# Latent attention: dividing by the softmax sums after the value product, with queries in the rows of that product

## The chip, the cores and the metric

One core of a Trainium2 chip runs the kernel. The metric is device time in microseconds (us); the runs of the kernel before are 2098.66, 2099.0 and 2093.48, their median 2098.66.

## The reference

Two layers, each with a half-step feed-forward block, a mixing stage and a second half-step feed-forward block, for 512 prompt positions and 64 sample positions, 576 tokens in all. The mixing stage projects the tokens to 1824 columns and runs three head groups on them: a chunk MLP (A), sliding-window attention (B), and latent attention (C, four heads). The change lies in C:

```python
def mla_attend(q_lat, q_pe, ckv, kpe, mask):
    s = (jnp.einsum('...qhr,...kr->...hqk', q_lat, ckv)
         + jnp.einsum('...qhp,...kp->...hqk', q_pe, kpe)).astype(jnp.float32) * ((C_NOPE + C_ROPE) ** -0.5)
    if mask is not None:
        s = jnp.where(mask, s, NEG)
    p = jax.nn.softmax(s, axis=-1).astype(ckv.dtype)
    return jnp.einsum('...hqk,...kr->...qhr', p, ckv)
...
    c = jnp.einsum('bthr,hrv->bthv', c_lat, w_uv).reshape(B, T, C_HEADS * C_V)
```

After it `h = h + concat(A, B, C) @ w_out`. The prompt's mask is block-causal in chunks of 64; the sample reads 256 cached positions and its own 64.

## The kernel before

All matrix products of the projections are made in three parts (high by high, low by high, high by low) of fp32r, with TensorE streaming 288 tokens a record. The feed-forward blocks hold most of the time. The change touches only `mixing`, of which each engine has one function (ScalarE L1195, TensorE L1595, VectorE L2361). All three walk the same list of steps, `PLAN` (L166), and each engine emits its own part of every step in that order; so an engine's instructions stand in the order of the list, and wait on counters of the others (`pe_did`, `act_did`, `dve_did`). A number after @ is the pair of PSUM banks, of four, that the step writes; a step waits until the last step in its pair has been read out (`tensor_needs`, L292).

The steps that matter here:
- z:x projects one slot of columns. w:x is ScalarE's making of the high part of a weight slot (L846), after which GpSimd makes the low part (L793). A:n and B:n are products of the output projection with the results of A and B; a B step is 24 TensorE records of 288 tokens. After the list comes `c_part` (L1745), 96 such records, the output projection of the latent attention's result.
- Latent attention runs in units 0 to 9: a tile of queries and a pair of heads. The tiles come in the order 1, 3, 4, 2, 0, with 2, 4, 3, 3 and 1 blocks of keys; tile 4 is the sample with 64 queries, the others have 128.
- MS:n, scores. TensorE makes them with queries in rows (L1699, L1704). VectorE masks (L2487), takes the maximum (L2494) and scales it (L2511). ScalarE takes the exponential for each of the two heads and their sums `den` (L1303). VectorE takes 1/den (L2515) and multiplies the probabilities by it (L2526).
- MT:n turns the probabilities, block by block, so that keys are in rows (TensorE L1713, one record per block and head); ScalarE copies them to one of two buffers `probsT` (L1206).
- MO:n, value product. For each block of keys and head the projected values `vc_tok` (128 keys by 64) stand in the array and the turned probabilities stream through, 128 queries a record, two records per product; the heads fill the two halves of the output's rows (L1736). ScalarE copies the result to `mixed_high` (L1206), VectorE takes the rest to `mixed_low` (L2536). The value product so comes out with channels in rows, as `c_part` reads it.
- The S, T, O steps do the same for the sliding window, with a division of their own that stays as it is.

```python
mm = nc.tensor.matmul(ps[p][64 * j:64 * j + 64, 0, 0:nq], vc_tok[0:n, row, c],
                      probsT[buffer_of(step)][0:n, (2 * k + j) * nq:(2 * k + j + 1) * nq],
                      start=k == 0, stop=k == len(keys) - 1)
```

Of the kernel before, what the change touches and what calls it, by code (L numbers as in the profile page):

```python
# [165 lines left out]
PLAN = """w:q0 z:k@0 sumx@3 w:q1 z:v@1 sw:k tw@2 w:q2 z:q0@0 rot:k z:q1@1 sw:q0 w:q3 w:va0 w:va1 sw:q1 tc@2 w:u0 rot:q0  # L166
z:q2@3 sw:q2 rot:q1 z:q3@1 rot:q2 sw:q3 w:u1 z:va0@0 tk@2 w:ckv w:cq0 rot:q3 z:va1@3 tva:0@0 S:0@2 z:u0@3 tv@1
tva:1@0 a:0@3 T:0@1 S:1@2 z:u1@0 w:cq1 O:0@1 w:cq2 T:1@2 S:2@0 z:ckv@3 T:2@2 w:kpe S:3@3 z:cq0@1 O:1@0 sumkv@3
T:3@1 S:4@2 O:2@3 a:1@1 z:cq1@0 w:qn T:4@3 S:5@1 O:3@2 z:cq2@0 O:4@3 T:5@1 S:6@2 z:kpe@0 sumq@3 tckv@1 O:5@0
T:6@3 w:A0 rkv@1 S:7@2 rep@1 qp@3 vc:0@0 rot:kpe@1 T:7@0 S:8@3 w:A1 qn:0@2 O:6@1 A:0@0 kn:0@3 T:8@2 S:9@1 O:7@0  # L170
A:2@2 qn:1@3 w:B0 A:1@1 rot:qp@0 T:9@2 tkpe@1 O:8@3 O:9@2 A:4@1 MS:0@2 vc:1@1 kn:1@3 w:B1 A:3@2 A:7@3 MT:0@0 w:B2
MS:1@1 B:0@0 A:6@3 MT:1@2 A:5@0 MS:2@3 MO:0@1 B:1@2 B:2@0 MT:2@1 MS:3@2 MO:2@1 B:3@0 MO:1@3 MT:3@2 w:B3 MS:4@1
B:4@3 MO:3@2 MT:4@1 MS:5@0 B:5@1 MT:5@2 MS:6@3 B:6@0 w:C0 MO:4@1 w:C1 MT:6@2 MS:7@3 B:7@1 MO:5@3 MT:7@2 MS:8@0
MO:6@2 MT:8@0 MS:9@2 MO:8@1 MO:7@0 MT:9@2 MO:9@0""".split()
# [2466 lines left out]
```

## Time and profile before

| | |
|---|---|
| runs | 2098.66, 2099.0, 2093.48 us |
| the profiled execution, its own time | 2092.16 us |
| its span | 2090.4 us |
| mean granted clock of TensorE | 0.994 |
| TensorE busy | 2048.2 us, 98% |
| VectorE, ScalarE, GpSimd busy | 1681.3, 977.5, 359.9 us |

The sum of a prediction is made against the profiled execution; of its 1.8 us beside the span the trace tells nothing. The first mixing stage lies at about 417 to 659 us of the span, the second at about 1446 to 1686 us. TensorE's clock has two levels; 1.00 in a row is 2.4 GHz and 0.50 is 1.2 GHz. A record's duration reaches past the start of the next one, since TensorE works in a pipeline; what a record costs is read from start to start.

### The profile page before, as it was taken

The numbers are of one execution on the slowest core, as the hardware profiler recorded it, in microseconds if no ns is written. First come the engines' busy times: TensorE is split into PE (matmuls) and PEld (weight loads), VectorE is DVE, ScalarE is ACT, GpSimd is POOL, SyncE is SP. The second block draws the span as 40 slices with busy tenths as digits, with TensorE's granted clock in tenths as the row PEclk, the third lists the DMA queues.
The fourth block names the chain that finished last, engine by engine and source line by source line (L and its number), as shares of the span: only waits on it lengthen the run. The fifth ranks groups of instructions, "written<-read, shape, count | busy, mean of one in ns | idle before, by whom it ended". The sixth has DMA issues, their size and how long they took to land. (4 is left out here: it accounts for less than half of the span.)

```text
span 2090.4 us, 41116 instructions
## 1 busy us (share of the span) xinstructions
PE 2048.2 (98%) x15435; PEld 1978.9 (95%) x15435; DVE 1681.3 (80%) x2481; ACT 977.5 (47%) x1772; POOL 359.9 (17%) x219
## 2 busy tenths in 40 slices
PE   9999999999999999999999999999999899999998
PEld 7999999999778999999989999999987699999998
DVE  5999998655655999998889999975565579999975
ACT  6544453324535544463465654533344464444532
POOL 0322200141110222200023222002402112222000
PEclk9999999999999999999999999999999999999999
DMA  4223323351111233232223322325312023332231
GB/s 131 94 88 100 96 75 105 94 128 42 46 41 62 86 95 100 91 92 85 77 82 101 100 80 87 103 76 128 94 45 64 31 62 101 100 93 85 83 105 64
DMA packets 236727, 178.35 MB, mean 85 GB/s; under 512 B 35808, under 2 KB 231616, under 8 KB 236608
## 3 DMA queue, kind: packets, MB, share of 16 engines
q1 hardware_dynamic: 231712, 170.36, 27.4%
q10 hardware_dynamic: 4896, 6.36, 1.1%
q8 instruction: 80, 1.31, 0.3%
q14 instruction: 39, 0.32, 0.1%
HBM read 170.12 MB, written 3.62 MB: 83 GB/s over the span
## 5 line engine op out<-in xcount | busy, mean ns | idle before, releaser
L1437 PE MATMUL pair<-t_parts,chunk_high 128*128 128x288 f32 x4592 | 919.2, 296 | 5.2 <-POOL chunk_low L799 2.5
L1437 PEld LDWEIGHTS pair<-t_parts,chunk_high 128*128 128x128 f32 x4592 | 738.9, 189 | 6.6 <-POOL chunk_low L799 3.2
L1437 PE MATMUL pair<-t_parts,chunk_low 128*128 128x288 f32 x2296 | 678.9, 296 | 0.0
L1437 PEld LDWEIGHTS pair<-t_parts,chunk_low 128*128 128x128 f32 x2296 | 432.7, 188 | 0.0
L799 POOL TENSOR_TENSOR chunk_low<-set_raw,chunk_high 128x512 fp32r<-128x512 f32 x164 | 237.5, 1458 | 871.5 <-ACT chunk_high L898 871.5
L898 ACT ACTIVATE chunk_high<-chunk_sum 128x512 fp32r<-128x512 f32 x328 | 203.9, 631 | 373.4 <-DVE chunk_sum L1990 190.3
L2002 DVE TENSOR_TENSOR chunk_low<-chunk_sum,chunk_high 128x512 fp32r<-128x512 f32 x328 | 214.4, 694 | 9.2 <-ACT chunk_high L898 1.9
L793 POOL TENSOR_TENSOR w_low<-raw,w_high 128x1024 fp32r<-128x1024 f32 (+2 forms) x48 | 115.0, 2402 | 619.6 <-ACT w_high L846 619.6
L1384 PE MATMUL pair<-hidden_high,w_high 128*128 128x288 f32 x896 | 192.1, 296 | 0.0
L1384 PE MATMUL pair<-hidden_high,w_low 128*128 128x288 f32 x896 | 191.9, 296 | 0.0
L1384 PE MATMUL pair<-hidden_low,w_high 128*128 128x288 f32 x896 | 191.6, 296 | 0.0
L846 ACT ACTIVATE w_high<-raw 128x896 fp32r<-128x896 f32 (+2 forms) x112 | 110.1, 984 | 140.5 <-PE pair L1570 56.0
L898 ACT ACTIVATE chunk_high<-set_raw 128x512 fp32r<-128x512 f32 x246 | 149.3, 620 | 0.0
L1384 PEld LDWEIGHTS pair<-hidden_low,w_high 128*128 128x128 f32 x896 | 144.5, 189 | 0.0
L1384 PEld LDWEIGHTS pair<-hidden_high,w_high 128*128 128x128 f32 x896 | 144.2, 189 | 0.0
L1384 PEld LDWEIGHTS pair<-hidden_high,w_low 128*128 128x128 f32 x896 | 144.2, 189 | 0.0
L1384 PE MATMUL pair<-x_high,w_high 128*128 128x288 f32 x480 | 105.1, 300 | 0.0
L1384 PE MATMUL pair<-x_high,w_low 128*128 128x288 f32 x480 | 102.7, 296 | 0.0
L1384 PE MATMUL pair<-x_low,w_high 128*128 128x288 f32 x480 | 102.6, 295 | 0.0
L1985 DVE TENSOR_TENSOR chunk_sum<-set_raw 128x512 f32<-128x512 f32 x82 | 82.4, 1005 | 14.9 <-PE pair L1437 14.5
L1021 ACT ACTIVATE chunk_high<-chunk_sum 128x512 fp32r<-128x512 f32 x64 | 39.1, 633 | 110.5 <-DVE chunk_sum L1910 95.2
L926 ACT ACTIVATE outputs<-outputs 128x576 f32<-128x576 f32 x88 | 59.4, 686 | 59.9 <-DVE outputs L2071 59.6
(300 smaller groups left out, 3732.6 us busy)
## 6 DMA issues: line engine op xcount, KB each, us to landing
set_raw<-in_w_up_dram SPq DMA_DIRECT2D x44, 1024.0 KB, 5.3
set_raw<-in_w_gate_dram SPq DMA_DIRECT2D x44, 1024.0 KB, 5.3
raw<-in_w_down_dram SPq DMA_DIRECT2D x64, 448.0 KB, 3.8
down_raw<-in_w_down_dram SPq DMA_DIRECT2D x16, 1024.0 KB, 5.4
raw<-in_w_in_dram SPq DMA_DIRECT2D x20, 512.0 KB, 4.0
raw<-in_w_in_dram SPq DMA_DIRECT2D x16, 256.0 KB, 3.8
raw<-in_w_out_dram SPq DMA_DIRECT2D x8, 512.0 KB, 3.5
raw<-in_w_out_dram SPq DMA_DIRECT2D x16, 256.0 KB, 4.0
```

Of the source, the lines that this page charges most:

```text
L793: nc.gpsimd.tensor_tensor(**low_of(s, slot_size(s))).then_inc(low_ready, 1)
L799: nc.gpsimd.tensor_tensor(out=cl[:, j], in0=set_raw[b][:, :, int(j == A12), 0:P], in1=ch[:, j].bitcast(F32), op=ALU.subtract).then_inc(low ...
L846: nc.scalar.activation(wh[s % RING][:, 0:n], raw[s % RAW][:, raw_from(s):raw_from(s) + n], ACT.Copy).then_inc(high_ready, 1)
L898: nc.scalar.activation(ch[:, j], src, ACT.Copy).then_inc(chunk_high, 1)
L926: nc.scalar.activation(g, g, ACT.Silu).then_inc(silu_done, 1)
L1021: nc.scalar.activation(ch[:, down_unit(g, j)], src, ACT.Copy).then_inc(d_high, 1)
L1384: mm = nc.tensor.matmul(ps[p][:, half, 0:HALF], w, x[:, half * HALF:(half + 1) * HALF], start=first and k == 0 and q == 0, stop=last and k ...
L1437: mm = nc.tensor.matmul(out, c[:, j, p, :], tr[p // 2][:, seat(p), x, t, :], start=p == 0 and n == 0, stop=p == KP - 1 and n == 2)
L1985: ins = nc.vector.tensor_tensor(cf[:, S1], block(b, 0, 1), block(b, 1, 1), ALU.add)
L2002: nc.vector.tensor_tensor(cl[:, j], src, ch[:, j].bitcast(F32), ALU.subtract).then_inc(low_by_dve, 1)
```

## The change

MS no longer multiplies the probabilities: VectorE writes 1/den to `inv_latent`, a column per unit and head, and is done. MT waits for ScalarE's exponentials instead of VectorE. MO has its operands exchanged: the turned probabilities stand in the array and 64 values stream through, with queries in rows and the two heads side by side in columns. ScalarE copies each head's half, multiplied by `inv_latent`, to one of two new tiles `o_tok`. A new step MU turns that tile (one TensorE record) and ScalarE and VectorE read it out as they read MO before. `PLAN` is another list: MU steps come in, and other steps and pairs are placed anew.

```diff
-MO:6@2 MT:8@0 MS:9@2 MO:8@1 MO:7@0 MT:9@2 MO:9@0""".split()
+MT:7@2 w:C0 MS:8@0 w:C1 MU:5@3 MO:6@2 B:7@1 MT:8@3 MS:9@2 MO:8@1 MU:6@3 MO:7@0 MT:9@2 MU:8@1 MO:9@0 MU:7@0 MU:9@2""".split()
...
+        "MT": lambda: [scalar_ops(f"MS:{arg}")[-1]],
+        "MU": lambda: [scalar_ops(f"MO:{arg}")[-1]],
...
-        "MT": lambda: [vector_ops(f"MS:{arg}")[-1]],
...
+        inv_latent = mix("inv_latent", [P, 2 * UNITS])
+        o_tok = [mix(f"o_tok{j}", [P, P]) for j in range(2)]
...
                     elif kind == "MO":
                         i, pair, t0, nq, keys = mla_unit(arg)
+                        dve_did(act, layer, vector_end(f"MS:{arg}"))
+                        turn = [x for x in MIX if x[:3] == "MO:"]
+                        at_n = turn.index(step)
+                        if at_n >= 2:
+                            pe_did(act, layer, "MU" + turn[at_n - 2][2:])
+                        for j in range(2):
+                            copy(o_tok[at_n % 2][0:nq, 64 * j:64 * j + 64], ps[p][0:nq, 0, 64 * j:64 * j + 64], f"{step}.{j}",
+                                 scale=inv_latent[0:nq, 2 * arg + j:2 * arg + j + 1])
+                    elif kind == "MU":
+                        i, pair, t0, nq, keys = mla_unit(arg)
                         copy(mh[:, 6 + pair, t0:t0 + nq], ps[p][:, 0, 0:nq], f"{step}.0")
...
-                        for k, (tile, n) in enumerate(keys):
-                            row = tile if i < 4 else (4, 5, 6)[k]
-                            for j in range(2):
-                                c = slice((2 * pair + j) * C_V, (2 * pair + j + 1) * C_V)
-                                mm = nc.tensor.matmul(ps[p][64 * j:64 * j + 64, 0, 0:nq], vc_tok[0:n, row, c],
-                                                      probsT[buffer_of(step)][0:n, (2 * k + j) * nq:(2 * k + j + 1) * nq],
-                                                      start=k == 0, stop=k == len(keys) - 1)
+                        for j in range(2):
+                            c = slice((2 * pair + j) * C_V, (2 * pair + j + 1) * C_V)
+                            for k, (tile, n) in enumerate(keys):
+                                row = tile if i < 4 else (4, 5, 6)[k]
+                                mm = nc.tensor.matmul(ps[p][0:nq, 0, 64 * j:64 * j + 64], probsT[buffer_of(step)][0:n, (2 * k + j) * nq:(2 * k + j + 1) * nq],
+                                                      vc_tok[0:n, row, c], start=k == 0, stop=k == len(keys) - 1)
+                    elif kind == "MU":
+                        i, pair, t0, nq, keys = mla_unit(arg)
+                        turn = [x for x in MIX if x[:3] == "MO:"]
+                        mm = nc.tensor.transpose(ps[p][:, 0, 0:nq], o_tok[turn.index(f"MO:{arg}") % 2][0:nq, :], ident[0:nq, 0:nq])
...
+                        if not swa:
+                            emit(nc.vector.reciprocal(inv_latent[0:nq, 2 * arg:2 * arg + 2], den[0:nq, 0:2]), names[n])
+                            continue
...
-                            emit(nc.vector.tensor_tensor(pr, pr, inv, ALU.mult), names[n])
```

TensorE at the end of the list, before: the last rows of the value product MO:5, then MT:7, MS:8 (two rows), MO:6, MT:8, MS:9 (two rows), MO:8, MO:7, MT:9 and MO:9. The step B:7 stands just ahead of these rows.

```order
L1736 MATMUL pair<-probsT_102,vc_tok 64x64 x6
L1713 MATMUL pair<-ident,probs 128x128 x6
L1699 MATMUL pair<-k_nopeT_132,q_nopeT_134 128x128 x2
L1704 MATMUL pair<-kpeT,q_peT 128x128 x2
L1736 MATMUL pair<-probsT_101,vc_tok 64x128 x6
L1713 MATMUL pair<-ident,probs 128x128 x2
L1699 MATMUL pair<-k_nopeT_133,q_nopeT_135 128x128 x2
L1704 MATMUL pair<-kpeT,q_peT 128x128 x2
L1736 MATMUL pair<-probsT_101,vc_tok 64x128 x2
L1736 MATMUL pair<-probsT_102,vc_tok 64x128 x6
L1713 MATMUL pair<-ident,probs 128x128 x2
L1736 MATMUL pair<-probsT_102,vc_tok 64x128 x2
```

The same place in the changed kernel, in two pieces. First from MS:7 to MO:6, behind which B:7 now stands (L1712 and L1717 are MS, L1749 is MO, L1726 is MT, L1754 is the new MU):

```order
L1712 MATMUL pair<-k_nopeT_134,q_nopeT_136 128x384 x2
L1717 MATMUL pair<-kpeT,q_peT 128x384 x2
L1749 MATMUL pair<-vc_tok,probsT_102 64x64 x6
L1726 MATMUL pair<-ident,probs 128x128 x6
L1712 MATMUL pair<-k_nopeT_133,q_nopeT_135 128x128 x2
L1717 MATMUL pair<-kpeT,q_peT 128x128 x2
L1754 MATMUL pair<-ident,o_tok_146 128x64
L1749 MATMUL pair<-vc_tok,probsT_101 128x64 x6
```

B:7 has moved from between MS:7 and MT:7 to between MO:6 and MT:8. Then, behind B:7, to the end of the list:

```order
L1726 MATMUL pair<-ident,probs 128x128 x2
L1712 MATMUL pair<-k_nopeT_134,q_nopeT_136 128x128 x2
L1717 MATMUL pair<-kpeT,q_peT 128x128 x2
L1749 MATMUL pair<-vc_tok,probsT_101 128x64 x2
L1754 MATMUL pair<-ident,o_tok_145 128x128
L1749 MATMUL pair<-vc_tok,probsT_102 128x64 x6
L1726 MATMUL pair<-ident,probs 128x128 x2
L1754 MATMUL pair<-ident,o_tok_146 128x128
L1749 MATMUL pair<-vc_tok,probsT_102 128x64 x2
L1754 MATMUL pair<-ident,o_tok_145 128x128
L1754 MATMUL pair<-ident,o_tok_146 128x128
```

Every value product is followed, one or more steps later, by its turn, and the list ends on two turns. ScalarE at the same place, before, from the exponentials of MS:8 on:

```order
L1303 ACTIVATE probs,den<-pair,neg_max,q_scale 128x128 x2
L1206 ACTIVATE mixed_high<-pair 128x128
L1206 ACTIVATE probsT_101<-pair 128x256
L1303 ACTIVATE probs,den<-pair,neg_max,q_scale 128x128 x2
L1206 ACTIVATE mixed_high<-pair 128x128 x2
L1206 ACTIVATE probsT_102<-pair 128x256
L1206 ACTIVATE mixed_high<-pair 128x128
```

And now, from the exponentials of MS:9 on:

```order
L1306 ACTIVATE probs,den<-pair,neg_max,q_scale 128x128 x2
L1209 ACTIVATE o_tok_146<-pair,inv_latent 128x64 x2
L1209 ACTIVATE mixed_high<-pair 128x128
L1209 ACTIVATE o_tok_145<-pair,inv_latent 128x64 x2
L1209 ACTIVATE probsT_102<-pair 128x256
L1209 ACTIVATE mixed_high<-pair 128x128
L1209 ACTIVATE o_tok_146<-pair,inv_latent 128x64 x2
L1209 ACTIVATE mixed_high<-pair 128x128 x2
```

Five copies stand between the last exponentials and the copy of `probsT` that MO:9 waits for, where two stood.

## Rows read from the trace of the kernel before

**Rows 1.** The page, part 1: busy time by engine.
```profile
PE 2048.2 (98%) x15435; PEld 1978.9 (95%) x15435; DVE 1681.3 (80%) x2481; ACT 977.5 (47%) x1772; POOL 359.9 (17%) x219
```
**Rows 2.** Waits of PE: line, releaser, us in total, times, longest.
```profile
PE pair L1713 <- DVE probs L2526: 10.5, 10, 2.0
PE pair L1713 <- issue: 4.0, 6, 1.1
...
PE pair L1384 <- DVE mixed_low L2536: 1.8, 2, 0.9
...
PE pair L1649 <- ACT ckvT L1206: 1.5, 2, 0.9
PE pair L1721 <- DVE z L2409: 1.4, 1, 1.4
PE pair L1721 <- ACT roots L1263: 1.4, 1, 1.4
...
PE pair L1736 <- ACT probsT L1206: 0.9, 2, 0.5
```
**Rows 3.** Timeline of PE, first layer, MO:5 to c_part: start, length in us.
```profile
631.37 0.71 PE L1736 MATMUL pair<-probsT,vc_tok 128*64 128x64 f32 x12
632.61 0.84 PE L1713 MATMUL pair<-ident,probs 128*128 128x128 f32 x6 [0.53 <-issue]
633.38 0.49 PE L1699 MATMUL pair<-k_nopeT,q_nopeT 64*128 64x128 f32 x4
...
644.70 0.82 PE L1384 MATMUL pair<-mixed_high,w_high 128*128 128x288 f32 x2 [0.89 <-DVE mixed_low L2536]
```
**Rows 4.** Timeline of PE, second layer, MS:8 to c_part.
```profile
1662.15 0.49 PE L1699 MATMUL pair<-k_nopeT,q_nopeT 64*128 64x128 f32 x4
...
1665.96 0.41 PE L1713 MATMUL pair<-ident,probs 128*128 128x128 f32 x2 [1.97 <-DVE probs L2526]
...
1667.17 1.09 PE L1736 MATMUL pair<-probsT,vc_tok 128*64 128x128 f32 x16
...
1672.36 0.82 PE L1384 MATMUL pair<-mixed_high,w_high 128*128 128x288 f32 x2 [0.89 <-DVE mixed_low L2536]
```
**Rows 5.** Timeline of PE: three stretches with full-precision records, first layer.
```profile
533.03 1.15 PE L1631 MATMUL pair<-mean_d,sq_tmp 128*128 128x1 f32 x10
...
574.64 0.33 PE L1682 MATMUL pair<-ckvT,w_uk 128*128 128x64 f32 x2
574.78 0.51 PE L1384 MATMUL pair<-mixed_high,w_high 128*128 128x288 f32 x2
...
599.82 1.09 PE L1736 MATMUL pair<-probsT,vc_tok 128*64 128x128 f32 x16
```
**Rows 6.** Timeline of PE, first layer: B:4 with the start of MO:3 behind it.
```profile
607.40 0.53 PE L1384 MATMUL pair<-mixed_high,w_high 128*128 128x288 f32 x2
...
610.78 0.44 PE L1736 MATMUL pair<-probsT,vc_tok 128*64 128x128 f32 x4
```
**Rows 7.** Timelines of PE (end of MS:6's scores) and ACT (exponentials, copies), both layers.
```profile
620.01 0.91 PE L1704 MATMUL pair<-kpeT,q_peT 32*128 32x384 f32 x4
...
623.84 0.20 ACT L1303 ACTIVATION_READ_ACCUMULATOR probs<-pair,neg_max,q_scale 128x1 f32 x1
...
641.11 0.44 ACT L1206 ACTIVATE mixed_high<-pair 128x128 fp32r<-128x128 f32 x2
642.67 0.38 ACT L1206 ACTIVATE probsT<-pair 128x256 f32<-128x256 f32 x1 [1.12 <-PE pair L1713]
...
1669.19 0.20 ACT L1303 ACTIVATION_READ_ACCUMULATOR probs<-pair,neg_max,q_scale 128x1 f32 x1
```
**Rows 8.** Windows: busy by engine (PE, PEld, DVE, ACT, POOL), then PEclk, DMA, GB/s.
```profile
638.00:644.00 6.00, 4.33 (x30) 2.71 (x27) 1.99 (x7) 1.88 (x9) 0.00 (x0) 0.50 0.01 3
1664.00:1666.00 2.00, 0.04 (x1) 0.07 (x2) 0.81 (x4) 1.16 (x5) 0.00 (x0) 1.00 0.00 0
1666.00:1668.00 2.00, 2.00 (x26) 1.59 (x26) 0.73 (x3) 0.38 (x1) 0.00 (x0) 1.00 0.00 0
```

More of the change, by code:

```diff
@@ L165 @@
 MLA_TILES = [1, 3, 4, 2, 0]
[L166 to L173, printed above, removed]
-MO:6@2 MT:8@0 MS:9@2 MO:8@1 MO:7@0 MT:9@2 MO:9@0""".split()
+PLAN = """w:q0 z:k@0 sumx@3 w:q1 z:v@1 sw:k tw@2 w:q2 z:q0@0 sw:q0 rot:q0 w:q3 rot:k z:q1@2 w:va0 tc@0 sw:q1 z:q2@3 w:va1
+w:u0 sw:q2 rot:q1 z:q3@1 rot:q2 tk@2 z:va0@0 sw:q3 w:u1 rot:q3 z:va1@3 tva:0@0 w:ckv S:0@2 w:cq0 z:u0@3 tv@2
+tva:1@1 a:0@3 w:cq1 T:0@1 S:1@0 w:cq2 z:u1@3 O:0@1 T:1@2 S:2@0 z:ckv@1 T:2@0 w:kpe S:3@2 z:cq0@1 sumkv@3 O:1@0
+T:3@1 S:4@2 O:2@3 a:1@1 z:cq1@0 T:4@3 S:5@1 O:3@2 z:cq2@0 w:qn O:4@3 T:5@1 S:6@2 z:kpe@0 sumq@3 w:A0 tckv@2 O:5@0
+T:6@3 rkv@1 S:7@2 rep@1 qp@3 vc:0@0 rot:kpe@1 T:7@0 S:8@3 qn:0@2 O:6@1 A:0@0 w:A1 kn:0@3 T:8@2 S:9@1 O:7@0 qn:1@3
+A:2@2 A:1@1 rot:qp@0 T:9@2 w:B0 w:B1 O:8@3 tkpe@1 O:9@2 A:4@0 MS:0@3 vc:1@1 kn:1@0 A:3@2 MT:0@3 MS:1@1 B:0@0
+A:6@2 A:7@3 MO:0@1 MT:1@2 A:5@0 w:B2 MU:0@2 MS:2@1 MO:1@3 B:1@2 B:2@0 MT:2@1 MS:3@2 MO:2@1 B:3@0 MU:2@1 MU:1@3
+w:B3 MT:3@2 MS:4@1 B:4@2 MT:4@1 MS:5@0 MO:3@3 B:5@1 MT:5@2 MS:6@3 B:6@2 MO:4@1 MT:6@2 MU:3@3 MU:4@1 MS:7@0 MO:5@1
+MT:7@2 w:C0 MS:8@0 w:C1 MU:5@3 MO:6@2 B:7@1 MT:8@3 MS:9@2 MO:8@1 MU:6@3 MO:7@0 MT:9@2 MU:8@1 MO:9@0 MU:7@0 MU:9@2""".split()
 MIX = [t.partition("@")[0] for t in PLAN]
@@ L213, in scalar_ops @@
     n = {"z": 0, "sumx": 1, "sumkv": 2, "sumq": 4, "tw": 1, "tv": 2, "tc": 2, "tk": 2, "tva": 2,
-         "rkv": 2, "tkpe": 2, "rep": 1, "a": 1, "kn": 1, "S": 5, "O": 1, "MS": 2, "MO": 1}.get(kind, 0)
+         "rkv": 2, "tkpe": 2, "rep": 1, "a": 1, "kn": 1, "S": 5, "O": 1, "MS": 2, "MO": 2, "MU": 1}.get(kind, 0)
     if kind == "vc":
@@ L231, in vector_ops @@
     n = {"z": 1, "sumx": 2, "sumq": 3, "tckv": 2, "tw": 1, "rot": 3, "a": 4, "qp": 1, "qn": 1,
-         "O": 1, "MO": 1, "A": 1, "B": 1}.get(kind, 0)
+         "O": 1, "MU": 1, "A": 1, "B": 1}.get(kind, 0)
     if kind == "z" and arg.startswith("cq"):
@@ L237, in vector_ops @@
     if kind == "MS":
-        n = 4 + (1 if mla_unit(arg)[0] < 4 else 0)
+        n = 3 + (1 if mla_unit(arg)[0] < 4 else 0)
     return [f"{step}.{k}" for k in range(n)]
@@ L265, in evacuated @@
     kind, arg = split(step)
-    if kind in ("z", "qp", "qn", "O", "MO", "A", "B"):
+    if kind in ("z", "qp", "qn", "O", "MU", "A", "B"):
         return "vector", f"{step}.0"
@@ L1300, in mixing @@
                         W = sum(n for _, n in keys)
-                        dve_did(act, layer, f"{step}.{len(vector_ops(step)) - 3}")
+                        dve_did(act, layer, f"{step}.{len(vector_ops(step)) - 2}")
                         for j in range(2):
@@ L1754, in c_part @@
                     if m == 0:
-                        dve_did(pe, layer, max((f"MO:{n}.0" for n in range(UNITS)), key=DVE_STEPS.index))
+                        dve_did(pe, layer, max((f"MU:{n}.0" for n in range(UNITS)), key=DVE_STEPS.index))
                     if m >= 4:
@@ L2519, in mixing @@
                         inv = inv_den[0:nq, 0:heads].unsqueeze(2).broadcast_to([nq, heads, W])
-                        if swa:
-                            emit(nc.vector.tensor_tensor(pr[:, 0:2], pr[:, 0:2], inv[:, 0:2], ALU.mult), names[n])
-                            n += 1
-                            emit(nc.vector.tensor_tensor(pr[:, 2:4], pr[:, 2:4], inv[:, 2:4], ALU.mult), names[n])
-                        else:
-                            emit(nc.vector.tensor_tensor(pr, pr, inv, ALU.mult), names[n])
+                        emit(nc.vector.tensor_tensor(pr[:, 0:2], pr[:, 0:2], inv[:, 0:2], ALU.mult), names[n])
+                        n += 1
+                        emit(nc.vector.tensor_tensor(pr[:, 2:4], pr[:, 2:4], inv[:, 2:4], ALU.mult), names[n])
                     elif kind == "O":
@@ L2532, in mixing @@
                                                      mh[:, js, t0:t0 + nq].bitcast(F32), ALU.subtract), names[0])
-                    elif kind == "MO":
+                    elif kind == "MU":
                         i, pair, t0, nq, keys = mla_unit(arg)
```

1 line of the change is left out of this document (removed).

## The prediction

> **What bounds the kernel.** I read the page first: TensorE is busy for 98% of the span, VectorE for 80%, ScalarE for 47% [rows 1]. So work taken from VectorE is worth only what TensorE waited for it, and every record added to TensorE counts, unless it falls into a wait. Then I read TensorE's waits. MT waits 10.5 us in ten places for the multiplication of the probabilities. "Issue" ahead of L1713 is 4.0 us in six: I take the two of 1.1 us for the sliding window's T:5 (one a layer) and the other 1.8 us for MT. The last value product waits 0.9 us for `probsT`, and `c_part` 1.8 us for `mixed_low` [rows 2]. Together 15.0 us in latent attention, 7.5 a layer: that is all the change can win there. The last view is the timeline of the end of each list. There TensorE has no projection product left to fill in, and from MS:8 to the first record of `c_part` it takes 644.70 - 633.38 = 11.3 us in the first layer [rows 3] and 1672.36 - 1662.15 = 10.2 us in the second [rows 4]. The reader should see in both that over half of the 15 us stands in this stretch.
>
> **The value product, MO.** Two products a key block, one per head, two records each. Before, 16 records take 1.09 us, 0.068 each [rows 5]: the two heads use different halves of the array's columns, 64 columns stand and 128 stream. After, 128 columns stand and 64 stream. No row has just this in a long series. Two rows bound it. Ten records with 128 standing columns and a single streamed one take 1.15 us, 0.115 each; that cannot be the streaming. Two records of exactly the new shape (L1682, 128x64) are followed after 0.14 us by the next product, 0.070 each, though behind a long record, under which their loads may hide [rows 5]. I take 0.115, since in MO no long record hides the loads; 0.070 stays as the lower end, at which the exchange costs nothing. In a layer the four tiles with 128 queries have 10 key blocks, so 10 x 2 pairs x 2 heads x 2 = 80 records: 80 x 0.047 = 3.8 us. Tile 4 stays at 64 standing columns; 0.
>
> The Trainium skill says, in TensorE: Matmul & The Clock Gate, section LDWEIGHTS, that a load of the standing operand costs time by its columns and not by its rows, 107 ns for 128 as I work it out from its formula. By it alone the exchange would cost 80 x (0.107 - 0.068) = 3.1 us a layer; the row with one streamed column agrees with it, the 0.14 us of the two records doesn't.
>
> **The turn, MU.** Ten records a layer. Six turns of MT take 633.38 - 632.61 = 0.77 us, 0.13 each [rows 3]; 1.2 us a layer, 0.6 of it up to MT:7. All of them stand beside other small steps, so no new change between kinds of products is paid.
>
> **VectorE and ScalarE.** VectorE loses a multiplication a unit, ScalarE gains two copies of 128x64 for one. Between them the steps A and B cover this, up to MS:7; at nothing, with this cover: behind MS:4, for instance, stands B:4, 610.78 - 607.40 = 3.4 us [rows 6]. From the end of the scores of a tile with three blocks (0.91 us from 620.01) to its last exponential's end (624.04) is 3.1 to 3.2 us [rows 7]. With a B step between MS and MT, MT then finds its exponentials done. I find this for MT:1 to MT:6, so the waits up to MT:7 vanish: 10.5 us less the four long ones of MT:8 and MT:9 (1.97, 1.0, 1.97, 1.88, of which [rows 4] show one), so 3.7, and the 1.8 us of issue; 5.5, or 2.8 a layer. The loads and low parts of the last weight slots come up to 8 us later; the first use of the feed-forward's first set lies behind three tiles of `c_part`, which covers that.
>
> **What takes their place.** B:7 stood between MS:7 and MT:7 and has moved behind MO:6. Between MS:7 and MT:7 is left only MO:5, 0.7 us [rows 3], against 3.2 us: a new wait of 2.5 us at MT:7.
>
> So from the start of latent attention to the end of MT:7, per layer: -3.4 (B:7 gone) - 2.8 + 2.3 (48 records of MO:0 to MO:3) + 0.6 + 2.5 = -0.8 us.
>
> **The end, from MS:8 on,** set out from 0:
> - MS:8 0.9, MU:5 0.1, MO:6 12 x 0.115 = 1.4, B:7 3.4: 5.8. MT:8 waits for nothing. MT:8 and MS:9 take 1667.17 - 1665.96 = 1.2 [rows 4]: 7.0.
> - MT:9 needs the exponentials of MS:9, which end 1669.39 - 1667.17 = 2.2 after it [rows 4, 7]: 9.2. MO:8, MU:6 and MO:7 are 2.0 us of work and lie within.
> - On ScalarE five small copies stand ahead of MT:9's copy. Two take 0.44 [rows 7], a further one about 0.2: 10.2. MT:9's copy takes 0.38: MO:9 starts at 10.7.
> - MO:9 four records and their drain, 0.6; two copies 0.5; MU:7 and MU:9 with drain 0.5; two copies 0.45; VectorE's rest and the signals 0.4: `c_part` starts at 13.1.
>
> Against 11.3 and 10.2 us: +1.8 and +2.9. So most of what the last turns and copies add lies on the path: MO to MU to `c_part` is a chain with nothing beside it.
>
> **Clock.** In the first layer the granted clock is 0.50 from 638 to 644 us, after a wait of 2 us. In the second, TensorE does 0.04 us of work from 1664 to 1666, has 1.00 all the same to 1668 [rows 8]. I leave what the clock costs in either layer as it was.
>
> **Sum.** First layer -0.8 + 1.8, second -0.8 + 2.9: together +3.1 us. The steps in front of latent attention keep their waits: 0. Ends: if MO's records cost 0.070, 160 x 0.045 = 7.2 us go: -4.1. Against the profiled execution: 2092.2 + 3.1 = 2095.3 us. This execution lies 6.5 us under the median of the runs, and of the four times two are near 2093 and two near 2099; their middle is 2095.6, and I forecast 2095.6 + 3.1, about 2098 us. A measurement tells this kernel from no change at about 0.3%, 6 us; so the forecast is: no change that counts.
>
> **Rivals.**
> - *Loads hidden.* The records of MO cost 0.070, as the two of L1682 do. Against it: the 0.115 of the short ones. -4.1 us, 2092.
> - *The front.* The list is new there too: w:A0 now stands ahead of the copies that `rep` (L1649) waits for, `w:qn` later. The waits in front are 2.2 us of T:5, 1.5 and twice 1.4 [rows 2], 6.5 in both layers. If they go, 3.1 - 6.5 = -3.4 us, 2092. Against it: `rep`'s successor waits for the same exponentials of S:7, so a wait taken from `rep` comes back one step later.
> - *Slower: the clock.* The new wait of 2.5 us at MT:7 is as long as the one after which the first layer ran at 0.50 for 6 us and more. If the clock falls there and stays down to the end of the list, the 7 us of work from MS:8 to MS:9, B:7 among them, take 14: one layer +7, 2106 us; both, 2113. It decides whether 0.50 stands in the windows before B:7. For it: [rows 8], first layer; against it: the second layer, where the same wait was followed by the full clock.
> - *The doing itself.* Should MT still wait for VectorE, through the pair or the list, the 5.5 us stay: +8.6, 2104. The order of the instructions speaks against it; I give it almost nothing.
>
> **Chances.** Forecast 0.53; loads hidden 0.14; the front 0.12; clock 0.14; the rest, among it two gains at once (-10.6 us) and a clock that doesn't fall at `c_part`, 0.07. Faster by over 0.3% are the two gains at once and the outer parts of each, 0.17; slower by over 0.3% are the clock and a little of the forecast's own scatter, 0.16; within, 0.67. The range: the scatter of the runs, 2092 to 2099, with -4.1 below gives 2088, and with one layer's clock above, 2106.
>
> **What would show it.** In the profile after: L1749 near 0.115 us a record; no wait of L1726 for VectorE; a wait of about 2.5 us ahead of MT:7 for ScalarE and one below 0.5 at MT:9; waits ahead of the last MO, the last MU and `c_part`; some 13 us from MS:8 to `c_part`. The forecast is wrong if MO's records come at 0.07, if 0.50 stands in front of B:7, or if the time between the end of the first product block and latent attention changes by over 2 us.

## The result and the profile after

The changed kernel takes 2110.82 us (median of 4 runs, 2107.51 to 2111.45), the kernel before 2096.87 us (4 runs, 2093.48 to 2099.0): a ratio of 1.0067, 95% interval 1.0053 to 1.0081, 14 us slower. The forecast was 2098 us with a range from 2088 to 2106: wrong, and above the range. The profiled execution took 2107.51 us with a span of 2105.3, against 2092.16 and 2090.4 before, so 14.9 us lie between the two traces.

The page, part 1, of the changed kernel: TensorE gained 16 us of busy time for 20 records, VectorE lost 10 [rows 1].

```profile
PE 2064.5 (98%) x15455; PEld 1998.1 (95%) x15455; DVE 1671.2 (79%) x2461; ACT 985.0 (47%) x1812; POOL 358.7 (17%) x219
```

TensorE's waits after (line, releaser, us in total, times, longest), to be held against [rows 2]:

```profile
PE pair L1726 <- ACT probs L1306: 4.5, 4, 2.0
...
PE pair L1726 <- issue: 2.5, 3, 1.2
...
PE pair L1668 <- ACT kpe_rep L1209: 2.1, 2, 1.0
PE pair L1397 <- DVE mixed_low L2550: 2.0, 2, 1.0
...
PE pair L1726 <- DVE probs L2540: 1.5, 1, 1.5
PE pair L1685 <- DVE uT L2425: 1.4, 2, 0.7
...
PE pair L1754 <- ACT o_tok L1209: 1.2, 2, 0.6
...
PE pair L1749 <- ACT probsT L1209: 1.0, 2, 0.5
...
PE pair L1726 <- DVE z L2425: 0.6, 2, 0.3
PE pair L1675 <- ACT probs L1298: 0.6, 2, 0.3
```

The 10.5 us for VectorE behind the scores are gone. In latent attention MT waits 4.5 us for the exponentials: 1.96 in each layer at MT:7 and 0.30 at MT:9. The last MO, the last MU and `c_part` wait as the walk had it. But L1685 and L1675 waited for nothing before, and L1668 has 2.1 us where the same line (L1655) had 0.9, while `rep`'s 1.5 us are gone [rows 2]: all of these are in front of latent attention (L1726 waits for VectorE there too, since T and MT share the line).

The timeline of PE in the first layer, MO:5 to `c_part` (start, length, operation), answers to [rows 3]:

```profile
630.81 1.30 PE L1749 MATMUL pair<-vc_tok,probsT 128*64 128x64 f32 x12
634.08 0.85 PE L1726 MATMUL pair<-ident,probs 128*128 128x128 f32 x6 [1.96 <-ACT probs L1306]
634.85 0.49 PE L1712 MATMUL pair<-k_nopeT,q_nopeT 64*128 64x128 f32 x4
...
635.90 2.75 PE L1749 MATMUL pair<-vc_tok,probsT 128*128 128x64 f32 x12
638.40 0.83 PE L1397 MATMUL pair<-mixed_high,w_high 128*128 128x288 f32 x2
...
643.65 0.38 PE L1726 MATMUL pair<-ident,probs 128*128 128x128 f32 x2
...
645.42 1.45 PE L1749 MATMUL pair<-vc_tok,probsT 128*128 128x64 f32 x12
647.17 0.41 PE L1726 MATMUL pair<-ident,probs 128*128 128x128 f32 x2 [0.30 <-ACT probs L1306]
...
648.33 0.66 PE L1749 MATMUL pair<-vc_tok,probsT 128*128 128x64 f32 x4 [0.52 <-ACT probsT L1209]
649.60 0.67 PE L1754 MATMUL pair<-ident,o_tok 128*128 128x128 f32 x2 [0.61 <-ACT o_tok L1209]
651.26 0.82 PE L1397 MATMUL pair<-mixed_high,w_high 128*128 128x288 f32 x2 [0.99 <-DVE mixed_low L2550]
```

The same twelve records of a value product stand there twice: 2.75 us at 635.90, behind the wait, and 1.45 us at 645.42. B:7, from 638.40 to 643.65, takes 5.25 us instead of 3.4. The windows say why. The last three columns are the granted clock, the DMA share and GB/s; the first four windows are of the first layer, the last two of the second:

```profile
636.00:640.00 4.00, 4.00 (x19) 4.00 (x20) 1.15 (x5) 3.17 (x9) 3.21 (x2) 0.50 0.02 4
640.00:644.00 4.00, 4.00 (x23) 3.83 (x22) 0.08 (x1) 0.00 (x0) 1.48 (x1) 0.65 0.21 58
...
648.00:652.00 4.00, 2.06 (x9) 1.56 (x10) 1.43 (x5) 1.46 (x7) 0.00 (x0) 0.71 0.00 0
652.00:656.00 4.00, 4.00 (x19) 4.00 (x18) 0.76 (x1) 0.55 (x2) 0.00 (x0) 0.50 0.00 0
...
1668.00:1672.00 4.00, 3.95 (x19) 3.08 (x19) 0.84 (x4) 2.06 (x4) 0.56 (x1) 0.50 0.00 0
...
1684.00:1688.00 4.00, 2.50 (x9) 2.13 (x10) 1.12 (x3) 0.94 (x4) 0.00 (x0) 0.50 0.01 4
```

Twice in each layer the clock goes down to 1.2 GHz (0.50) in place of 2.4: behind the wait at MT:7, and behind the small waits at the end of the list, where `c_part` begins. In four of the six windows TensorE is busy for 3.95 us or more of the 4, so the low clock lies over work. In the kernel before, the low clock of the first layer lay for the most part over windows in which TensorE had less to do (2.33 us of 4 here):

```profile
640.00:644.00 4.00, 2.33 (x16) 1.16 (x12) 1.30 (x5) 1.85 (x8) 0.00 (x0) 0.50 0.00 0
```

Cut at the same records (first token sum, MS:0, MS:8, first record of `c_part`, and the feed-forward's first record behind it), the layers look so, in us, with four of the experiments told below. The shifted kernel has other steps between MS:0 and MS:8 than the rest, so for it only the sum of the two middle stretches compares:

| stretch, layer | before | after | idle products at MT:7 | B:7 back | shifted | before, idle products |
|---|---|---|---|---|---|---|
| token sums to MS:0, first | 152.9 | 154.5 | 155.9 | 154.5 | 154.3 | 153.0 |
| the same, second | 152.9 | 154.8 | 154.8 | 154.9 | 152.9 | 154.1 |
| MS:0 to MS:8, first | 63.0 | 61.9 | 61.9 | 63.2 | 57.0 | 63.1 |
| second | 63.0 | 62.5 | 61.9 | 63.2 | 57.0 | 63.1 |
| MS:8 to `c_part`, first | 11.3 | 16.4 | 13.2 | 14.7 | 15.3 | 11.0 |
| second | 10.2 | 16.7 | 13.2 | 14.7 | 15.3 | 11.0 |
| `c_part`, first | 14.3 | 15.2 | 15.6 | 15.6 | 12.9 | 12.8 |
| second | 13.9 | 14.9 | 15.3 | 14.2 | 12.9 | 12.8 |

From before to after: front +1.6 and +1.9, MS:0 to MS:8 -1.2 and -0.5, the end +5.1 and +6.5, `c_part` +0.9 and +1.0: 15.3 us. What is left of the 14.9 is -0.4: a low clock in the first 40 us of this execution, 1.1, against 1.5 us less between the two layers.

### The profile page after: what moved, and what is told of

The parts are those of the page before. It is cut to its first block and busy times, and to the rows that moved or that the text cites. A ratio compares the mean times of both kernels' runs of the same rounds, so it can differ in the third digit from the quotient of the medians.

```text
span 2105.3 us, 41202 instructions
## 1 busy us (share of the span) xinstructions
PE 2064.5 (98%) x15455; PEld 1998.1 (95%) x15455; DVE 1671.2 (79%) x2461; ACT 985.0 (47%) x1812; POOL 358.7 (17%) x219
## 3 DMA queue, kind: packets, MB, share of 16 engines
q8 instruction: 80, 1.31, 0.3%
## 5 line engine op out<-in xcount | busy, mean ns | idle before, releaser
L2001 DVE TENSOR_TENSOR chunk_sum<-set_raw 128x512 f32<-128x512 f32 x82 | 83.9, 1023 | 14.2 <-PE pair L1450 13.8
```

The costliest lines, as they stand in the source:

```text
L2001: ins = nc.vector.tensor_tensor(cf[:, S1], block(b, 0, 1), block(b, 1, 1), ALU.add)
```

## The experiments

The theory: the walk along the end of the list was right at the full clock (13.1 us), the clock then took some 3 us of each end and more of `c_part`, and the front took the rest. The rivals: the clock would fall there anyway; the new division costs it all; the front is only clock.

**The front.** The changed kernel with the old order up to A:4.

```diff
-PLAN = """w:q0 z:k@0 sumx@3 w:q1 z:v@1 sw:k tw@2 w:q2 z:q0@0 sw:q0 rot:q0 w:q3 rot:k z:q1@2 w:va0 tc@0 sw:q1 z:q2@3 w:va1
...
+PLAN = """w:q0 z:k@0 sumx@3 w:q1 z:v@1 sw:k tw@2 w:q2 z:q0@0 rot:k z:q1@1 sw:q0 w:q3 w:va0 w:va1 sw:q1 tc@2 w:u0 rot:q0 z:q2@3
...
```

> The changed kernel with the old list up to A:4, its own from there on. Theory 1 (the new front of the list costs time): the stretch from the token sums (418.5) to MS:0 (573.0) was 1.6 us longer in the first layer and 1.9 us in the second than before; it goes back, 3.4 us of 2107.5, and the tail is as it was: about 2104 in the profiled execution, 2107 by the median. Theory 2 (the front differs by chance or through the changed steps behind it): the stretch stays 1.6 and 1.9 us longer and the time stays at 2107 to 2111.

Measured: 2106.76 us (4 runs, 2106.15 to 2106.88), 4.1 us less. In the changed kernel's trace the front has four new waits in the first layer:

```profile
473.64 0.74 PE L1675 MATMUL pair<-ident,vT 128*128 128x128 f32 x5 [0.31 <-ACT probs L1298]
475.64 1.36 PE L1685 MATMUL pair<-w_sT,va_tok 128*64 128x128 f32 x20 [0.71 <-DVE uT L2425]
486.07 0.63 PE L1726 MATMUL pair<-ident,probs 128*128 128x128 f32 x4 [0.68 <-issue]
504.80 0.95 PE L1726 MATMUL pair<-ident,probs 128*128 128x128 f32 x7 [0.31 <-DVE z L2425]
```

They are 2.0 us, of which 1.8 remain up to T:5 and 1.6 at MS:0. The trace names VectorE for half of them (`uT`, which step a:0 needs, and `z`). From 440 to 460 us VectorE is busy for 16.9 us where it was busy for 13.4, since `rot:q0`, `rot:k` and `tc` now come to it in another order; with the old order it is busy for 13.5 us there and the four waits are gone. That it is this reordering and none of the others in the front wasn't tested by itself. Yet in the profile of this experiment the stretch takes 154.0 and 154.5 us, hardly less, record for record as before up to `rep` (L1662), then 1.1 us later in the first layer, and 1.5 in the second from T:6 on. One window at that place, of the kernel before and then of the experiment:

```profile
544.00:548.00 4.00, 3.56 (x19) 2.67 (x17) 1.50 (x4) 3.85 (x12) 0.00 (x0) 1.00 0.51 131
```

```profile
544.00:548.00 4.00, 4.00 (x20) 3.85 (x20) 1.11 (x4) 3.31 (x11) 0.00 (x0) 0.72 0.48 131
```

The same program piece at the same times, once with the full clock and once not: behind its two waits of 1.1 and 1.4 us [rows 2] the clock falls in some executions and not in others. The profiled execution of the kernel before had it in neither layer, which may be a part of why it lies 5 us under the median. Over all traces of this document, the old front takes 152.9 to 153.0 us in 12 of 20 layers and 154.0 to 155.3 in the other eight; the new one takes 154.5 to 156.2 in eight layers and never less. So a front is to be judged by its waits, or by many traces, not by its length in one; by the median, this one costs 4 us.

**The clock behind MT:7.** Fifteen idle products (a product into the PSUM pair that MT:7 will overwrite) keep TensorE at work in the wait.

```diff
+                    if step == "MT:7":
+                        act_did(pe, layer, evacuated(before_in_pair(step))[1])
+                        for _ in range(15):
+                            nc.tensor.matmul(ps[p][:, 0, 0:HALF], wh[1][:, 0:P], mh[:, 0, 0:HALF], start=True, stop=True)
```

> The changed kernel with 15 idle products of 128x288 put on TensorE in the wait ahead of MT:7 (about 2.0 us, the length of the wait); they write the bank pair that MT:7 overwrites and delay nothing. Theory 1 (the clock falls because of this wait): 0.50 no longer stands in the windows between MT:7 and MT:8 in either layer, MO:6 and B:7 run at full speed, and 3.1 + 3.3 + 0.7 = 7 us go: about 2100.5 profiled, 2104 by the median. Theory 2 (the clock falls through the exchanged operands or the turns, with the wait as a bystander): 0.50 stands there still and the time stays within 2 us.

Measured: 2100.82 us (10 runs, 2098.92 to 2102.91), 10.0 us less, 3 more than expected: adding work won 10 us. The timeline of PE, first layer, with the idle products (L1619):

```profile
632.45 2.24 PE L1619 MATMUL pair<-mixed_high,w_high 128*128 128x288 f32 x15
...
636.32 1.55 PE L1753 MATMUL pair<-vc_tok,probsT 128*128 128x64 f32 x12
...
648.43 0.82 PE L1397 MATMUL pair<-mixed_high,w_high 128*128 128x288 f32 x2 [1.10 <-DVE mixed_low L2554]
```

MO:6 takes 1.55 us in place of 2.75, B:7 its 3.3, and MS:8 to `c_part` takes 13.15 us in one layer and 13.18 in the other: the 13.1 us of the walk, at full clock. The traces account for 3.3 + 3.5 + 0.6 us of the gain (the last is MT:7 itself in the second layer). The other 2.6 no trace shows; they would fit that the profiled execution of the changed kernel lies 3.3 us under its own median. What the edit doesn't touch is `c_part`: 15.6 and 15.3 us, at half clock behind the small waits.

**B:7 back where it was,** between MS:7 and MO:5; else the changed kernel.

```diff
-w:B3 MT:3@2 MS:4@1 B:4@2 MT:4@1 MS:5@0 MO:3@3 B:5@1 MT:5@2 MS:6@3 B:6@2 MO:4@1 MT:6@2 MU:3@3 MU:4@1 MS:7@0 MO:5@1
...
+MS:5@0 MO:3@3 B:5@1 MT:5@2 MS:6@3 B:6@2 MO:4@1 MT:6@2 MU:3@3 MU:4@1 MS:7@0 B:7@3 MO:5@1 MT:7@2 w:C0 MS:8@0 w:C1 MU:5@3
...
```

> The changed kernel with B:7 back between MS:7 and MO:5, where it stood before. Theory 1 (the place of B:7 makes wait and fall of the clock): the 2.0 us wait ahead of MT:7 is gone, one of 0.5 to 0.9 us stands ahead of MT:8, the 7 us of half clock are gone; per layer -2.0 + 0.7, together -2.6 - 7 = about -9.6 us: 2098 profiled, 2101 by the median. Theory 2 (the end of the list is so thin without B:7 that the clock falls all the same, only later): the waits change as said, but 0.50 stands from about MT:9 or MT:8 on, and only 3 to 6 us are won.

Measured: 2106.05 us (5 runs, 2105.23 to 2106.09), 4.8 us less; the second theory by its size. A wait of 2 us now stands at MT:8, and the clock falls behind it. But it is another wait than the one at MT:7. These are lines of the timelines of ScalarE, VectorE and PE in the first layer, then PE's windows:

```profile
639.56 1.05 ACT L849 ACTIVATE w_high<-raw 128x1024 fp32r<-128x1024 f32 x1
640.50 0.22 ACT L1209 ACTIVATE mixed_high<-pair 128x64 fp32r<-128x64 f32 x1
...
640.85 0.23 DVE L2550 TENSOR_TENSOR mixed_low<-pair,mixed_high 128x64 fp32r<-128x64 f32 x1 [0.99 <-ACT mixed_high L1209]
...
641.18 0.66 PE L1726 MATMUL pair<-ident,probs 128*128 128x128 f32 x2 [1.98 <-ACT o_tok L1209]
```

```profile
640.00:644.00 4.00, 2.82 (x14) 2.08 (x15) 0.72 (x3) 1.51 (x5) 3.19 (x2) 0.54 0.00 0
644.00:648.00 4.00, 3.74 (x19) 3.34 (x18) 0.78 (x4) 2.52 (x11) 0.00 (x0) 0.50 0.81 261
648.00:652.00 4.00, 2.40 (x9) 1.84 (x10) 1.41 (x4) 1.03 (x5) 0.00 (x0) 0.50 0.01 2
```

The exponentials of MS:8 are done at 639.66, so for them MT:8 would have waited some 0.5 us, as expected. The other 1.5 us it waits for its pair of banks, 3, which MU:5 wrote: ScalarE copies that product only behind the weight slot of w:C1 (1.05 us), and VectorE's rest of it ends at 641.08, 0.1 us ahead of MT:8. The trace puts the wait down to a copy of ScalarE that ran at the same time. So putting B:7 back took away the wait at MT:7 and made one of the same length out of a pair and the place of w:C1. What B:7's place is worth by itself this run doesn't show; it does show that a wait of 2 us is followed by the low clock here too, with less of B behind it.

**What the division costs in the kernel before.** Multiplication left out (the probabilities are not divided), MT waits for the exponentials.

```diff
+        "MT": lambda: [scalar_ops(f"MS:{arg}")[-1]],
...
-        "MT": lambda: [vector_ops(f"MS:{arg}")[-1]],
...
+                        if not swa:
+                            continue
                         own(names[n])
```

> The kernel before, its own list, with the multiplication by 1/den left out (the latent attention's values are not divided) and MT waiting for the exponentials. It shows what taking the multiplication off the path is worth by itself. Theory 1 (its waits are worth what the rows said): the waits ahead of MT fall by up to 0.6 to 1.45 us each, in all 3.7 + 1.8 + 4 x 0.65 = about 8 us: 2084 profiled, -8 against before. Theory 2 (a wait that is shortened comes back at the next step, or the weights' steps on ScalarE take it): under 4 us.

Measured: 2086.64 us (4 runs, 2085.17 to 2089.41), 10.3 us less, where 8 were expected. So of the 15.0 us of waits in latent attention about 10 could be won in this order, clock included; and the new records cost 5 us a layer by the forecast, 5.6 as measured below, which is as much or more.

**The new division alone,** on the old order with MU put in (the diff is against the list of the kernel before).

```diff
-MO:6@2 MT:8@0 MS:9@2 MO:8@1 MO:7@0 MT:9@2 MO:9@0""".split()
+MO:6@2 MT:8@0 MS:9@2 MO:8@1 MU:6@3 MO:7@0 MT:9@2 MU:8@1 MO:9@0 MU:7@3 MU:9@2""".split()
```

> The new division alone, on the order of the kernel before, with the MU steps put in (the order that the change searched is left out). If the division alone is nearly free and the new order brought the loss (front of the list, the wait ahead of MT:7, B:7 at half clock), this runs within 3 us of the kernel before: 2096 to 2100. If the new division itself costs what was lost (full-precision loads and the longer end walk at whatever clock), it runs at 2104 or more.

Measured: 2105.28 us (6 runs, 2104.37 to 2106.7): the second case. MS:0 to `c_part` takes 78.7 and 78.5 us against 74.4 and 73.3, `c_part` 15.3 and 15.5. Part of it is the records (5.6 us a layer, as the two shifted kernels show below). The waits, in turn, went only in part; timeline of PE, first layer:

```profile
597.73 1.07 PE L1726 MATMUL pair<-ident,probs 128*128 128x128 f32 x8 [1.18 <-issue]
...
639.83 0.41 PE L1726 MATMUL pair<-ident,probs 128*128 128x128 f32 x2 [1.07 <-ACT probs L1306]
```

Between MS and MT the old order has too little work for the exponentials themselves, whoever divides. The clock is 0.50 to 0.60 from 640 to 652 us and 0.63 or less from 1674 to 1686.

**Idle products in all waits of the end,** on the changed kernel with the old front (15 at MT:7, and 4, 4 and 7 ahead of MO:9, MU:9 and `c_part`), **and the same in the kernel before** (15, 14, 3 and 6 ahead of MT:8, MT:9, MO:9 and `c_part`).

```diff
+            def fill(layer, n, done):
+                engine, name = evacuated(done)
+                (act_did if engine == "scalar" else dve_did)(pe, layer, name)
+                for _ in range(n):
+                    nc.tensor.matmul(ps[3][:, 0, 0:HALF], mh[:, 0, 0:P], mh[:, 0, 0:HALF], start=True, stop=True)
...
+                        fill(layer, 7, 'MU:6')
```

> The changed kernel with the old order up to A:4, 15 idle products in the wait ahead of MT:7 and 4, 4 and 7 idle ones in the waits ahead of the last MO, the last MU and the first product of c_part. Theory (two independent losses: front of the list 4 us, clock 10 us, and a third of about 1 us per layer at the head of c_part): 2110.8 - 4 - 10 - 2 = about 2095, c_part's first four blocks back to 14.0 us per layer, no 0.50 in either tail. Rival (the gains overlap, or the clock falls elsewhere as soon as it is held up here): 2099 or more, with a window of 0.50 further on.

> The kernel before, with 15, 14, 3 and 6 idle products in its own waits ahead of MT:8, MT:9, the last MO and c_part: what a held clock is worth with the division where it was. Theory (the same wait of 1.97 us also lets the clock fall in the old kernel, but with little work behind it): 1.1 us won in the first layer's tail, up to 0.7 in each c_part, so 2094 to 2096, and a gain far below the 10 us that the same edit gave the changed kernel. Rival (holding the clock up is worth the same in either kernel, so the clock is no reason for the loss): 2087 or so.

Measured: 2095.78 us (12 runs, 2093.5 to 2099.5) for the first, 15 us under the changed kernel, where 2095 was expected: front and clock add up. The idle products aren't free, and the clock isn't held everywhere: from MS:8 to `c_part` the first layer takes 15.0 us, with 0.59 from 643 to 647 us, and the second 14.1, at full clock, against 13.2 with MT:7's wait alone filled. And 2091.7 us (10 runs, 2089.87 to 2093.01) for the second, 5.3 us under the kernel before. `c_part` takes 12.8 to 13.0 us in both. So a held clock is worth 11.0 us to the changed kernel with the old front (2106.76 less 2095.78) and 5.3 to the one before, more there than the 1 to 3 expected, and far from equal. By these medians the 14 us of the change are 4.1 of front, 5.7 of clock (11.0 less 5.3) and 4.1 that stay when front and clock are set right (2095.78 less 2091.7). The window of the kernel before with idle products, first layer, over the end of the list:

```profile
633.00:645.00 12.00, 11.02 (x99) 9.30 (x100) 5.35 (x17) 4.34 (x15) 0.00 (x0) 1.00 0.16 55
```

**The B products later.** Instead of idle products, real ones: B:0 goes behind MS:2 in place of MS:1, B:1 behind MS:3 in place of MS:2, and B:2 to B:5 go two units later, B:5 behind MS:7; pairs and weight steps are placed anew with them; B:6 fills the wait ahead of MT:8 and B:7 the one behind MT:9.

```diff
-MT:7@2 w:C0 MS:8@0 w:C1 MU:5@3 MO:6@2 B:7@1 MT:8@3 MS:9@2 MO:8@1 MU:6@3 MO:7@0 MT:9@2 MU:8@1 MO:9@0 MU:7@0 MU:9@2""".split()
...
+B:3@0 MT:5@1 MS:6@2 B:4@0 MO:4@3 MT:6@1 MU:3@0 MU:4@3 w:C0 MS:7@2 MO:5@1 B:5@0 MT:7@1 w:C1 MS:8@3 MU:5@2 MO:6@0 B:6@1
+MT:8@2 MS:9@0 MO:8@3 MU:6@1 MO:7@2 MT:9@0 B:7@3 MU:8@1 MO:9@2 MU:7@0 MU:9@3""".split()
```

> The changed kernel with the old order up to A:4 and, behind it, the B products one unit later than before the change (B:0 behind MS:2 to B:5 behind MS:7), B:6 between MS:8 and MT:8, B:7 between MT:9 and MO:9, so that no wait of 2 us is left ahead of MT:7. Theory (the half clock behind the long wait is most of the loss): no L1726 wait for ScalarE of 2 us, 1.00 in the windows of both tails, median 6 to 10 us below the old-front kernel's 2106.8, so 2097 to 2101. Rival (the clock falls from the density of the short products themselves, wait or no wait): a window of 0.50 in both tails all the same and 2104 to 2107. Second rival (the B products are needed where they were, and waits come back up to MT:7): the stretch from MS:0 to MS:8 grows by over 3 us per layer, 2105 or more.

Measured: 2087.18 us (6 runs, 2085.7 to 2088.42), ratio to the kernel before 0.9956 (0.9944 to 0.9968): 9.9 us faster than before the change, 23.6 than after it, and 10 under the bottom of what was expected. The windows over both ends:

```profile
628.00:644.00 16.00, 14.52 (x113) 12.88 (x111) 5.49 (x16) 7.23 (x26) 2.40 (x1) 1.00 0.22 67
1652.00:1668.00 16.00, 14.36 (x111) 12.84 (x111) 5.67 (x17) 7.13 (x25) 2.39 (x1) 1.00 0.21 67
```

Neither is below 1.00, nor are the windows over the two `c_part`s (644 to 658 us and 1668 to 1682), and MS:0 to `c_part` takes 72.24 us in both layers, 2.8 less than at full clock in the changed order (61.9 + 13.15), the wait at MT:7 and two small ones being filled.

**Is that the order or the division?** The same order without MU on the kernel before (the diff is against its list); and the shifted kernel with the changed kernel's front.

```diff
-MS:1@1 B:0@0 A:6@3 MT:1@2 A:5@0 MS:2@3 MO:0@1 B:1@2 B:2@0 MT:2@1 MS:3@2 MO:2@1 B:3@0 MO:1@3 MT:3@2 w:B3 MS:4@1
...
+w:B2 MS:2@1 MO:1@3 B:0@0 MT:2@1 MS:3@2 MO:2@1 B:1@0 w:B3 MT:3@2 MS:4@1 B:2@0 MT:4@1 MS:5@3 MO:3@2 B:3@0 MT:5@1 MS:6@2
+B:4@0 MO:4@3 MT:6@1 w:C0 MS:7@2 MO:5@1 B:5@0 MT:7@1 w:C1 MS:8@3 MO:6@0 B:6@1 MT:8@2 MS:9@0 MO:8@3 MO:7@2 MT:9@0 B:7@3
+MO:9@2""".split()
```

> The order of the shifted kernel (B products one unit later, B:6 and B:7 in the last two waits), without the MU steps, on the kernel before, whose division stands in front of the turn. Theory (the shift gained by covering waits, whichever the division, and the new division still costs its full-precision records): from the shifted kernel's 72.24 us from MS:0 to c_part go 3.6 us of MO and some 1.5 us of MU, and up to 2 us of waits for VectorE come: 67 to 69 us, c_part 12.9, median 2079 to 2085, so below the 2087.2 of the shifted kernel. Rival (without the new division the turn still waits for VectorE behind each scores step, and the shift pays only with the division moved out of the way): over 71 us from MS:0 to c_part and 2087 to 2093.

> The shifted order from A:4 on, with the changed kernel's own front of the list. Theory (front and rest add up): the front costs here what it cost with the other tail, 4 us, so 2091 (2089.5 to 2092.5), with 154.5 us from the token sums to MS:0. Rival (most of those 4 us were a lower clock that the earlier waits brought on, and go with it): 2088 or less.

Measured: 2089.44 us (6 runs, 2086.93 to 2091.65) with the old division, in the rival's range: its MS:0 to `c_part` takes 72.4 and 73.6 us. What it doesn't pay in MO and MU it waits: in the first layer, at full clock in both, TensorE is busy for 64.6 us where it is busy for 70.2 with the new division, and idle for 7.7 where it is idle for 2.0. Two of its waits, in the second layer:

```profile
1654.47 0.84 PE L1713 MATMUL pair<-ident,probs 128*128 128x128 f32 x6 [1.67 <-DVE mixed_low L2536]
...
1664.31 0.66 PE L1713 MATMUL pair<-ident,probs 128*128 128x128 f32 x2 [1.88 <-DVE probs L2526]
```

With the changed kernel's front the shifted kernel takes 2091.08 us (8 runs, 2090.07 to 2091.86), 3.9 more than without, as expected, though the two ran on different chips; against all 12 runs of the shifted kernel (2088.2, below) it is 2.9. So the front costs about as much with this end as with the other. To tell the two divisions apart, both shifted kernels ran again on one chip:

> The shifted kernel with the new division a second time, now on one chip with the shifted kernel of the old division. Theory (with the B products one unit later the new division pays, since the old one still waits for VectorE in the tail): 2087 again, 1.5 to 3 us below the other, the two sets of runs hardly overlapping. Rival (the 2.3 us between them lay between two chips): both within 1 us.

> The shifted kernel with the old division a second time, beside the one with the new division. Theory: 2089 to 2090, and above the other. Rival: within 1 us of it.

Measured: 2089.36 us (6 runs, 2086.93 to 2090.64) with the new division and 2088.43 us (5 runs, 2087.11 to 2089.78) with the old one. The rival holds. Over both times the medians are 2088.2 (12 runs) and 2088.5 (11 runs): in this order the new division is worth nothing that these runs can tell. All of the gain over the kernel before, 8 to 10 us, is the order's. The traces do differ: with the new division MS:0 to `c_part` takes 72.24 or 72.25 us in all six layers traced, and with the old one 72.4, 73.6, 73.6 and 75.4, the longer ones with a low clock behind waits of 1.67 or 1.88 us (0.61 to 0.70 over 4 us). Why that doesn't reach the medians stays open.

## Why the prediction was wrong, point by point

Two steps failed, both of them terms put at nothing: what the clock costs (8.2 us by the traces, 5.7 by the medians) and the front of the list (3.4 us by the traces, 4 by the median). The rest of the sum came within 0.5 us, in part by luck.

- *The value product.* L1749 has 8 records from 592.55 to the next product at 593.46, 0.114 each, and 16 from 603.02 to 604.83, 0.113:

```profile
592.55 1.10 PE L1749 MATMUL pair<-vc_tok,probsT 128*128 128x64 f32 x8
593.46 0.51 PE L1397 MATMUL pair<-mixed_high,w_high 128*128 128x288 f32 x2
...
603.02 2.00 PE L1749 MATMUL pair<-vc_tok,probsT 128*128 128x64 f32 x16
604.83 0.38 PE L1397 MATMUL pair<-mixed_high,w_high 128*128 128x288 f32 x1
```

  The size is right for the tiles with 128 queries, 0.115 taken, and "loads hidden" is out. The reason is not, or not alone, that 128 columns stand. Tile 4 was put at 0 ("stays at 64 standing columns"), yet its twelve records of one and the same shape went from 0.71 us, 0.059 each [rows 3], to 1.27 in MO:4 and 1.31 in MO:5 (the line at 630.81), 0.105 to 0.109 each. Before, the two heads stood in different halves of the array's columns, and the trace has their records starting two by two, 6 to 7 ns apart. Now both heads use the same columns, and the records start one by one. The first 0.03 us of MO:5 before has two records, the first 0.06 us now has one:

```profile
631.37 0.28 PE L1736 MATMUL pair<-probsT,vc_tok 128*64 128x64 f32 x2
...
630.81 0.24 PE L1749 MATMUL pair<-vc_tok,probsT 128*64 128x64 f32 x1
```

  So the change gave up that TensorE ran two heads side by side, a term the prediction had in view ("the two heads use different halves") and didn't price. With it MO costs 4.5 us a layer at full clock (3.4 for the tiles with 128 queries, 1.1 for tile 4), not 3.8. How much of the 3.4 is width and how much pairing no run separates. The Trainium skill's 107 ns from TensorE: Matmul & The Clock Gate, section LDWEIGHTS, is 6 ns under what the records with 128 standing columns show. By the same formula 64 columns are 53 ns, an estimate; tile 4's records took 59 before and take 105 to 109 now, so columns alone don't set a record's cost here.
- *MU, VectorE and ScalarE.* Right: no MT waits for VectorE's multiplication any more, and MS:0 to MS:8 fell by 1.2 us in the first layer (the forecast had 0.8 up to the end of MT:7) and by 0.5 in the second, where MT:7 at half clock adds 0.6. That the sum is near is partly luck. Taken from start to start, the terms are -4.0 for B:7 (-3.4 forecast), -2.8 for the waits and MT (-2.8), +1.9 for MO:0 to MO:3 (+2.3), +1.1 for tile 4 (0), +0.6 for MU (+0.6) and +2.0 for the wait at MT:7 (+2.5).
- *The new wait at MT:7.* 2.5 us forecast, 1.96 measured. From the end of MS:7's scores to its last exponential are 3.1 us, as forecast; what stands in between, MO:5, takes 1.3 us and not 0.7. So MO:5's extra cost lies in the wait, and only MO:4's lengthens the layer.
- *The walk along the end.* Right: 13.1 us forecast, 13.15 and 13.18 measured once the clock was held. Inside it two small misses cancel: MO:9 starts at 10.35 and not 10.7, and the rest takes 2.8 and not 2.4. At one clock the step from MS:0 to `c_part` thus costs 75.05 - 73.25 = 1.8 us a layer; the sum said 3.1 for both together. But the sum set a walk at full clock against 11.3 us of the first layer, of which 1.1 is half clock, and so took those 1.1 us off without saying so. At one clock its own terms give 4.2, against 3.6 measured.
- *"I leave what the clock costs in either layer as it was."* This step failed, and it is most of the error. Of the 16.4 and 16.7 us of the end, 3.3 and 3.5 are half clock, and 0.6 more at MT:7; `c_part`, which takes 12.9 us at full clock, takes 15.2 and 14.9. That is 11.7 us. In the kernel before it is 1.1 us in the first end and 1.4 and 1.0 in the two `c_part`s, 3.5. So 8.2 of the 15 us. The rival named the mechanism and the place, and its sign (0.50 before B:7) is there in both layers of this trace, and in both of the experiment with the old front; but it had 0.14, and it priced 7 us a layer where the end lost 3.3, because the clock came back inside B:7. It left out `c_part`, where the clock falls a second time and costs 4.4 us in both layers. The argument against it, that the second layer had kept its clock behind the same wait, was one execution of something that varies.
- *"The steps in front of latent attention keep their waits: 0."* This failed too: +1.6 and +1.9 us, 4 by the median. The prediction knew that the list was new there and looked only for waits that might go. What it said of `rep` held: its 1.5 us are gone, and L1668, a step later, waits 1.2 more.
- *The base.* The sum was set on a time 3 us above the profiled execution, rightly: over 59 runs in these comparisons the kernel before has a median of 2097.0 (2092.1 to 2099.9).

So 3.6 (measured at full clock, 3.1 forecast), 8.2 of clock and 3.4 of front make 15.2, against 15.3 between the cuts. The medians with idle products give the clock less, 5.7 us, and the rest 4.1; the idle products' own cost and what varies from execution to execution lie between the two. What else stays open is the 2.6 us of the idle products' gain that the two profiled executions don't show, and why 1.5 us less lie between the layers.

## What to carry to other kernels

Price a wait on a nearly full TensorE by what runs behind it as well as by its length: 2 us of idling cost 2 us and up to 5 us more of half clock, and it was worth 10 us to fill it even with idle work. Hold back independent products for the last waits of a stage, each a unit or two later, before changing how the stage computes: here the order brought 8 to 10 us and the new algorithm, once ordered, nothing. Before exchanging the operands of a product, look whether products run side by side, and price what is lost with that. And where a change brings a newly searched order, compare it over its whole length; the part that has no business with the change cost 4 us.
